# Issuing an expert's down product behind the next expert's gate-up product, in a fused decoder layer with 32 experts

## What is computed

```python
def expert_step(acc, params):
    wgu, bgu, wd, bd, g = params
    hgu = xt @ wgu + bgu
    gate = jnp.minimum(hgu[:, :D_EXPERT], SWIGLU_LIMIT)
    up = jnp.clip(hgu[:, D_EXPERT:], -SWIGLU_LIMIT, SWIGLU_LIMIT)
    y = ((up + 1.0) * (gate * jax.nn.sigmoid(SWIGLU_ALPHA * gate))) @ wd + bd
    return acc + g[:, None].astype(y.dtype) * y, None
```

## Time and profile before

| | |
|---|---|
| median of three runs | 1309.89 us (1307.11 to 1310.67) |
| span of the profiled execution, first to last instruction | 1304.8 us |
| median above that span | 5.1 us |
| PE busy | 1151.2 us (88%) |
| DVE busy, ACT busy | 207.3 us (16%), 210.2 us (16%) |
| read from memory over the span | 435.74 MB, 335 GB/s |
| mean granted TensorE clock | 0.937 of full speed |

### The profile page before, as it was taken

The page is one execution under the profiler, slowest core; times in us unless marked ns, Lnnn a source line. Parts: engine busy times, 40 slices in busy tenths (PEclk is TensorE's granted clock), DMA queues, the critical chain, the costliest instruction groups (busy, mean ns, idle before and its releaser), DMA issues.

```text
span 1304.8 us, 15767 instructions
## 1 busy us (share of the span) xinstructions
PE 1151.2 (88%) x6100; PEld 472.1 (36%) x6100; DVE 207.3 (16%) x424; ACT 210.2 (16%) x356; POOL 18.6 (1%) x68
## 2 busy tenths in 40 slices
PE   7999999878888888888888888888888888888884
PEld 6675444433333333333333333333333333333331
DVE  1301222231111111111111111111111111111112
ACT  2363230211111111111111111111111111111111
POOL 1010000000000000000000000000000000000000
PEclk9999999979899989999998999899989998999897
DMA  9913324339999999999999999999999999999970
GB/s 336 354 65 129 128 85 160 147 113 386 399 399 397 398 401 393 395 405 401 396 400 395 393 395 395 409 397 387 399 402 397 396 403 403 405 394 399 401 308 33
DMA packets 86624, 437.04 MB, mean 335 GB/s; under 512 B 7704, under 2 KB 7760, under 8 KB 53744
## 3 DMA queue, kind: packets, MB, share of 16 engines
q1 hardware_dynamic: 84880, 434.19, 83.8%
q10 hardware_dynamic: 1424, 1.57, 0.5%
q0 software_dynamic: 304, 1.06, 0.2%
HBM read 435.74 MB, written 1.06 MB: 335 GB/s over the span
## 4 chain that ended last, share of the span: by engine, by line
PE 88%; DVE 7%; ACT 4%; issue 1%; DMA 0%; DVEq 0%; SPq 0%; ACTq 0%
PE bank L984 35%; PE bank L1010 22%; PE bank L818 6%; PE bank L958 5%; PE bank L815 4%; PE bank L949 4%; PE bank L901 2%; PE bank L912 2%; DVE gates L758 2%; DVE gates L760 2%; DVE gates L754 2%; PE bank L1001 2%; ACT gates L545 2%; ACT gates L547 1%; PE bank L978 1%
## 5 line engine op out<-in xcount | busy, mean ns | idle before, releaser
L984 PE MATMUL bank<-ring,gates 128*64 128x512 f32 x2048 | 460.1, 596 | 0.0
L1010 PE MATMUL bank<-ring,gates 128*64 128x512 f32 x1024 | 286.9, 724 | 22.0 <-ACT gates L547 22.0
L984 PEld LDWEIGHTS bank<-ring,gates 128*64 128x64 f32 x2048 | 140.9, 137 | 252.1 <-issue 244.9
L754 DVE TENSOR_SCALAR gates<-bank 128x512 f32<-128x512 f32 x32 | 22.1, 691 | 862.0 <-PE bank L984 862.0
L1010 PEld LDWEIGHTS bank<-ring,gates 128*64 128x64 f32 x1024 | 84.0, 166 | 205.3 <-issue 174.7
L1001 PE MATMUL bank<-ident,gates 128*128 128x128 f32 x128 | 21.1, 289 | 95.9 <-DVE gates L760 95.9
L818 PE MATMUL bank<-ring,colsT 128*128 128x512 f32 x192 | 85.0, 596 | 0.0
L545 ACT ACTIVATE gates<-gates 128x512 f32<-128x512 f32 x32 | 20.1, 629 | 398.7 <-DVE gates L754 398.7
L958 PE MATMUL bank<-gates,scatter_w 64*128 64x512 f32 x264 | 65.6, 615 | 0.7 <-ACT gates L550 0.7
L550 ACT ACTIVATE gates<-bank 128x512 f32<-128x512 f32 x32 | 19.1, 597 | 290.2 <-PE bank L1010 290.2
L949 PEld LDWEIGHTS bank<-onehot,qkT 128*128 128x128 bf16 x1584 | 49.1, 99 | 28.7 <-issue 26.0
(11 more groups left out here) (168 smaller groups left out, 501.2 us busy)
## 6 DMA issues: line engine op xcount, KB each, us to landing
ring<-in_w_gate_up_dram SPq DMA_DIRECT2D x256, 1024.0 KB, 9.0
ring<-in_w_down_dram SPq DMA_DIRECT2D x128, 1024.0 KB, 7.1
ring<-in_w_in_dram SPq DMA_DIRECT2D x10, 2048.0 KB, 18.9
ring<-in_w_out_dram SPq DMA_DIRECT2D x1, 4096.0 KB, 13.7
ring<-in_w_proj_sb_dram SPq DMA_DIRECT2D x1, 2048.0 KB, 7.6
ring<-in_w_proj_moba_dram SPq DMA_DIRECT2D x1, 2048.0 KB, 13.4
resid<-in_x_dram SPq DMA_DIRECT2D x2, 512.0 KB, 3.7
bias<-u_scratch POOLq DMA_DIRECT2D x1, 1024.0 KB, 12.6
```

What stands on the lines that cost most here:

```text
L754: V.tensor_scalar(gate_t, bank[4][:, :], SWIGLU_LIMIT, None, ALU.min).then_inc(gate_rd, 1)
L984: ins = mm(bank[4 + i][SLOTS * c:SLOTS * (c + 1), :], xeT[:, k, :], ring[:, k, i * D + c * CH:i * D + (c + 1) * CH], start=False, stop=k = ...
L1010: ins = mm(bank[6][SLOTS * c:SLOTS * (c + 1), :], rows, ring[:, KD + s, j * D + c * CH:j * D + (c + 1) * CH], start=k == 0, stop=k == KD - 1)
```

## The change

The down product of expert e-1 is issued behind the gate-up product of expert e. PE first does the gate-up products of experts 0 and 1, then down 0, gate-up 2, down 1 and so on; after the loop come the transposes, scatter and down product of the last expert. Scatter now lags two experts behind. The transposes of weights and of h go to bank 7, which the gather uses too, and PE waits for the copy out of it (`gT_rd`, `hT_rd`) after two further steps of gate-up. `slot_used` is split into `gu_used` and `dn_used`, and SP loads gate-up of e+1 and then down of e. On DVE, the spreading of the token weights (`slot_weights`) is for expert e-1; on ACT the copies of weights and of hT are for e-1 too, ahead of the sigmoid of e. The table load of ACT's sigmoid stands once ahead of the loop, no longer in it. The number of matmuls and of loads is the same; two MEMSETs are gone.

```diff
+            def load_gate_up(e, done, first=0):
+                for k in range(first, KD):
+                    sp.wait_ge(gu_used, (e + done) * KD + (k + 1 - KD))
+                    load_slot(e, k)
+
+            def load_down(e, done):
+                for q in range(RING - KD):
+                    sp.wait_ge(dn_used, (e + done) * (RING - KD) + (q + 1 - RING + KD))
+                    load_slot(e, KD + q)
+
+            def experts(done):
+                load_gate_up(1, done)
+                with sp.Fori(1, E - 1) as e:
+                    load_gate_up(e + 1, done)
+                    load_down(e, done)
+                load_down(E - 1, done)
...
             def experts(done):
-                with act.Fori(0, E) as e:
...
+                nc.scalar.activation(stat[:, 63:64], stat[:, 6:7], ACT.Sigmoid)
+                gate_sigmoid(done)
+                with act.Fori(1, E) as e:
+
+                    token_weights(e + (done - 1))
+                    hidden_columns(e + (done - 1))
+                    gate_sigmoid(e + done)
+                    expert_rows(e + (done - 1))
...
+                with dve.Fori(1, E - 1) as e:
                     one_hots(e + 1).then_inc(onehot_rd, 1)
...
+                    slot_weights(e - 1, done)
+                    hidden(e, done, True)
+                    next_tokens(e + 1, done)
...
+            def expert(g, scatters, more):
+
+                gate_up(g, (0, 1))
+                if scatters:
+                    scatter_rows(g - 2)
+                weight_columns(g - 1)
+                gate_up(g, (2, 3))
+                pe.wait_ge(gT_rd, g)
+                hidden_columns(g - 1)
+                gate_up(g, (4, 5))
+                pe.wait_ge(hT_rd, g)
+                if more:
+                    gather(g + 2)
+                gate_up(g, (6, 7))
+                if scatters:
+                    pe.wait_ge(y_rd, g - 1)
+                down(g - 1)
...
+                gate_up(done, (0, 1, 2, 3, 4))
+                gather(done + 2)
+                gate_up(done, (5, 6, 7))
+                expert(done + 1, False, True)
+                with pe.Fori(2, E - 1) as e:
+                    expert(e + done, True, True)
+                expert(done + (E - 1), True, False)
+                pe.wait_ge(gT_rd, done + (E - 1))
+                hidden_columns(done + (E - 1))
+                scatter_rows(done + (E - 2))
+                pe.wait_ge(hT_rd, done + E)
+                weight_columns(done + (E - 1))
+                down(done + (E - 1))
+                scatter_rows(done + (E - 1)).then_inc(scattered, 1)
```

More of the change, by code:

```diff
@@ L245, in hybrid_layer @@
         xe_rd = sem("xe_rd")
-        slot_used = sem("slot_used")
+        gu_used = sem("gu_used")
+        dn_used = sem("dn_used")
         gate_rd = sem("gate_rd")
@@ L259, in hybrid_layer @@
         pass_step = sem("pass_step")
+        spread_rd = sem("spread_rd")
         pass_base = sem("pass_base")
@@ L325, in _, with another_pass @@
                 load_slot(0, s)
[L327 to L335, removed]
+            def load_gate_up(e, done, first=0):
[12 more added lines that the diff above has]
+                load_down(E - 1, done)
+            def another_pass(r):
+                load_gate_up(0, r * E)
+                load_down(0, r * E)
+                experts(r * E)
+            experts(0)
+            more_passes(sp, another_pass)
             sp.wait_ge(out_rd, 1)
@@ L535, in _, with token_weights @@
             nc.scalar.activation(pieces[2], res2, ACT.Copy).then_inc(piece_rd, 1)
-            def experts(done):
-                with act.Fori(0, E) as e:
[L540 to L550, removed]
+            def token_weights(g):
+                act.wait_ge(gT_ps, g + 1)
+                nc.scalar.activation(stat[:, 61:62], stat[:, 6:7], ACT.Sigmoid)
+                nc.scalar.activation(scatter_w[:, :, :], bank[7][:, 0:T].rearrange("p (t s) -> p t s", t=NT),
+                                     ACT.Copy).then_inc(gT_rd, 1)
@@ new lines, in hidden_columns, with gate_sigmoid, expert_rows @@
+            def hidden_columns(g):
+                act.wait_ge(hT_ps, g + 1)
+                nc.scalar.activation(hT[:, :, :], bank[7][:, :].rearrange("p (c s) -> p c s", c=4), ACT.Copy
+                                     ).then_inc(hT_rd, 1)
+            def gate_sigmoid(g):
+                act.wait_ge(gate_rd, g + 1)
+                nc.scalar.activation(sig_t, gate_t, ACT.Sigmoid, scale=SWIGLU_ALPHA).then_inc(sig_rd, 1)
+            def expert_rows(g):
+                act.wait_ge(dn_used, g * (RING - KD) + (RING - KD))
+                nc.scalar.activation(y_t, bank[6][:, :], ACT.Copy).then_inc(y_rd, 1)
@@ new lines, in experts @@
+                next_tokens(0, done)
+                one_hots(1).then_inc(onehot_rd, 1)
+                hidden(0, done, False)
+                next_tokens(1, done)
+                with dve.Fori(1, E - 1) as e:
+                    one_hots(e + 1).then_inc(onehot_rd, 1)
+                    slot_weights(e - 1, done)
+                    hidden(e, done, True)
+                    next_tokens(e + 1, done)
+                slot_weights(E - 2, done)
+                hidden(E - 1, done, True)
+                dve.wait_ge(gT_ps, done + (E - 1))
@@ L764, in experts @@
+                slot_weights(E - 1, done)
                 dve.wait_ge(scattered, passes + 1)
@@ L960, in scatter, with gate_up @@
                 return ins
+            def gate_up(g, ks):
+                if ks[0] == 0:
+                    pe.wait_ge(sel_rd, g + 1)
+                    pe.wait_ge(xe_rd, g + 1)
+                    for i in range(2):
+                        for c in range(2):
+                            mm(bank[4 + i][SLOTS * c:SLOTS * (c + 1), :], expert_sel[:, :],
+                               bgu[:, i * D + c * CH:i * D + (c + 1) * CH], start=True, stop=False)
+                for k in ks:
+                    pe.wait_ge(slot_in[k], g * 16 + 16)
+                    for i in range(2):
+                        for c in range(2):
+                            ins = mm(bank[4 + i][SLOTS * c:SLOTS * (c + 1), :], xeT[:, k, :],
+                                     ring[:, k, i * D + c * CH:i * D + (c + 1) * CH], start=False,
+                                     stop=k == KD - 1)
+                    ins.then_inc(gu_used, 1)
@@ new lines, in scatter_rows, with weight_columns, hidden_columns @@
+            def scatter_rows(g):
+                pe.wait_ge(y_rd, g + 1)
+                pe.wait_ge(gT_rd, g + 1)
+                return scatter()
+            def weight_columns(g):
+                pe.wait_ge(weighted_rd, g + 1)
+                for t in range(NT):
+                    ins = tp(bank[7][:, t * P:(t + 1) * P], onehot_g[:, t, :], ident[:, :])
+                ins.then_inc(gT_ps, 1)
+            def hidden_columns(g):
+                pe.wait_ge(h_rd, g + 1)
+                for c in range(4):
+                    ins = tp(bank[7][:, c * P:(c + 1) * P], h_t[:, c * P:(c + 1) * P], ident[:, :])
+                ins.then_inc(hT_ps, 1)
@@ new lines, in down @@
+            def down(g):
+                pe.wait_ge(hT_rd, g + 1)
+                for s in range(RING - KD):
+                    pe.wait_ge(slot_in[KD + s], g * 16 + 16)
+                    for j in range(2):
+                        k = 2 * s + j
+                        rows = hT[:, k % 4, SLOTS * (k // 4):SLOTS * (k // 4) + SLOTS]
+                        for c in range(2):
+                            ins = mm(bank[6][SLOTS * c:SLOTS * (c + 1), :], rows,
+                                     ring[:, KD + s, j * D + c * CH:j * D + (c + 1) * CH], start=k == 0,
+                                     stop=k == KD - 1)
+                    ins.then_inc(dn_used, 1)
@@ L962, in experts @@
             def experts(done, r):
-                base = 0 if r is None else r * (E + 1)
-                gather(base + 1)
+                gather(done + 1)
                 if r is None:
@@ L972, in experts @@
                                stop=True)
[L973 to L1013, removed]
```

64 lines of the change are left out of this document (30 added, 34 removed).

## The result

The changed kernel takes 1242.83 us in the median of four runs (1241.16 to 1244.82), the kernel before 1308.5 in the same comparison: ratio 0.950, 95% interval 0.948 to 0.952. The forecast was 1238 in a range of 1222 to 1272. The profiled execution took 1241.16 us with a span of 1239.3.

A forecast was written before the change was run, and what follows sets the result against it. PE bounded the kernel before, and the transfers at 420 GB/s would bound it after. First landing 286.3 + 926.3 of queue + 1.8 + 15.3 + 3 of allowances gave a span of 1233, plus 5.1 made 1238 us, range 1222 to 1272.

The forecast's parts named there:

- the prediction's check of 32.0: PE's time per expert before, summed as 18.4 + 4.4 stall + 7.0 down product + 2.2 clock, against 31.58 us in the chain.
- PE's own pace afterwards: PE's time per expert after the change without waits for weights: 18.4 + 1.0 + 7.0 = 26.4 us.
- first reissue: The first load issued again into a freed ring slot, at 281.5 us as before, landing 4.8 us later at 286.3.
- behind the down product: What follows the last expert's down product until the span ends, 15.3 us, taken over from the kernel before.
- lower clock at the end: Allowance of 2 us for the last slot and scatter running at PE's lower clock.
- the 926.3 us for 389.0 MB at 420 GB/s: Time for the remaining loads after the first has landed, at the rate read over 817:843 where a backlog stood.
- The bounds of 410 and 425 GB/s for this case: Rates assumed for transfers as the bound, giving 949 to 915 us of queue and 1222 to 1262 us; chance 74%.
- the 5.1 us carried over: Median time of 1309.89 less profiled span of 1304.8 before, added to the forecast span to give the time.
- The limit at 398 GB/s (1): Rival: transfers give no more than 398 GB/s over long stretches, so 977 us of queue and 1289 us; 8%.
- the new wait of PE (2): Rival: PE waits x us per expert for bank 7 or xeT, hidden below 3.6; 7% part gain, 3% no change.
- The clock (3): Rival: idle pieces between slots hold PE at 1.2 GHz, hidden up to 7 us per expert, 1360 at 14; 5%.
- That the wait for h might remain (4): Rival excluded beforehand: h(e-1) is made beside the down product of e-2 and needed after four slots of next gate-up.

The follow-up runs named there:

- removing the clock's part alone: Kernel before with 12 filling matmuls, result thrown away, on PE in front of its wait for h, nothing moved: 1247.70 us, ratio 0.953.
- the comparison run: The changed kernel once more, unaltered, on the same chip as the runs with 8 KiB down pieces and moved b_down matmuls: 1245.10 us, ratio 0.950.
- Half of the filling: Kernel before with 6 filling matmuls in place of 12 on PE in front of its wait for h: 1309.94 us, ratio 1.000.

## Why the prediction was right

**PE was the bound before, not the transfers:** right, shown by the halved bytes. The stall and the clock had about the sizes given: removing the clock's part alone gave 1.98 us per expert against 2.2 worked out. The 9.92 us of the expert read was the longest of a pattern of four that repeats in the chain before (8.4, 9.9, 8.8, 8.7; mean 9.0). The mean is 1.9 above 7.1, and with 1.9 for 2.2 most of the gap between the prediction's check of 32.0 and 31.58 closes.

**PE's own pace afterwards:** 25.87 us, forecast 26.4. In the chain the down product takes 6.87 instead of 7.0 and the transposes of h 0.59 instead of 1.0; the 0.2 for changing pattern in that 1.0 had no row behind it and none shows it. The ways through bank 7 and to xeT stayed hidden. Only the second expert, which has no down product in front of it, waited 3.6 us for xeT; the prediction did not see that.

**The transfers become the bound, and the sum goes along the queue:** right. The sum, term by term:

| Term | forecast | measured |
|---|---|---|
| first reissue | 281.5 | 281.6 |
| last landing (1213.9 + 8.2; forecast with 1 of allowance) | 1212.6 + 1 | 1222.1 |
| last slot | 1.8 | 1.9 |
| behind the down product | 15.3 | 15.3 |
| lower clock at the end | 2 | 0 |
| span | 1233 | 1239.3 |

The last issues of SP's queue and their landings, then the last down product:

```profile
L315 SPq DMA_DIRECT2D ring<-in_w_down_dram x4: 368/374/382, 1206.3 to 1213.9; - x4
...
DMA to landing us min/median/max: 8.1/8.2/8.2
```

```profile
1216.80 7.16 PE L1049 MATMUL bank<-ring,gates 128*64 128x512 f32 x32
```

The term that was mis-sized is the 926.3 us for 389.0 MB at 420 GB/s; it took 935.8. The rate over the long run was 418, which is 4.3 us. A part of this is the mix: the window of the earlier trace rows held some 8 gate-up and 2 to 3 down loads, more gate-up than the 2 to 1 of an expert, and down loads go at 410 against 421; that mix would give 419, and the last GB/s stays open. The thin stretch at 303 to 317 cost 2 x (1 - 61/418) + 12 x (1 - 377/418) = 2.9 where 1 was allowed. The rest, some 2 us, lies in the last loads, when the queue is no longer full: the last three us to 1222 carry 340, 160 and 29 GB/s (not tested by itself). The 2 us for a lower clock at the end were not needed. The misses partly cancel, 6.3 us of span in all. The bounds of 410 and 425 GB/s for this case had no rows behind them; down loads by themselves do go at 410, and 425 was not reached (418 over 400:1150, 422 over 1180:1200).

**That the gain is more than the pace:** right. 31 x (31.58 - 30.14) = 45 us of the 65.5 us of span come from the pace. The other 21 come from the end: from the last issue to the end of the span it was 46.1 us before (1258.7 to 1304.8) and is 25.4 now (1213.9 to 1239.3), since the last loads are used as they land.

**From the span to the time:** the 5.1 us carried over was not an overhead. The profiled run after took 1241.16 for a span of 1239.3, and a run of the kernel before with halved bytes 1310.77 for 1309.0: 1.9 and 1.8. The other 3.3 of the 5.1 are there because the profiled execution before was of the quick variant, with b_down at full clock, and its median was not. The changed kernel's profiled execution was of the same quick variant, and its median of four is 3.5 above its span. So 1.6 of the 6.3 us were hidden by luck, and the median was missed by 4.8. The first reissue at 281.5 came true for the same reason; in the comparison run it was at 285.5.

**Rivals.** The limit at 398 GB/s (1) and the new wait of PE (2) are out by the queue's 418 and PE's 25.87. The bound of 3.6 us below which (2) calls a wait hidden doesn't follow from its own sum: 295 + 31 x (26.4 + x) + 25 passes the forecast span of 1233 at x of about 3, since PE's path has its own start and end; the 7 us of (3) likewise become 6. The clock (3) did the opposite: granted full speed, 1.00, over 305:1215. That the wait for h might remain (4) was rightly excluded. A rival that the prediction does not have is SP: in the changed kernel its issues fill nearly the whole period (see the last section). It is out too. The loads land 17.7 to 26.6 us behind their issue, so some 7 or more loads stand in the queue; if SP's issuing were the bound, they would not pile up. A quarter fewer pieces (8 KiB for down) shortened the period by 1% only. The clock was forecast at 0.97 or more and is 1.00 over 400:1150.

What the prediction lacked is how little of the change is needed. It took 5.7 us per expert off PE (31.58 to 25.87), of which the queue lets 1.4 through, and the fall of the clock alone was 2.0.

## What to carry to other kernels

When an engine paces the transfers, the mean rate and the busy share of the DMA engines say nothing about their limit: read the rate where a backlog stands, multiply by all bytes, and set that beside the engine's pace without its stalls. If the two are close, a cheap filling of the stall can be worth as much as a reordering; but here it had to fill nearly the whole wait, and half of it was worth nothing. Once the queue bounded, three things made the time: when its first reissue leaves, its rate with the pieces it is given, and what stands behind its last landing. And the loads have to be reordered together with the work that frees their slots.

## What the runs showed of the hardware

Issuing a load can itself take long. SP needed 0.38 us for a down load before, and in the changed kernel, with 17.7 to 26.6 us from issue to landing, that is some 7 to 10 loads of 2.5 us in flight, the issues on SP took (min/median/max in ns, window 400:1180):

```profile
L310 SPq DMA_DIRECT2D ring<-in_w_gate_up_dram x208: 840/1030/5094, 410.5 to 1176.6; - x104
...
L315 SPq DMA_DIRECT2D ring<-in_w_down_dram x104: 849/4018/4181, 400.3 to 1178.0; - x104
...
DMA to landing us min/median/max: 17.7/22.6/26.6
```

So the chain of the changed kernel names SPq with 47% of the span, more than PE. In the turn from 862.75 us on, the eight gate-up issues last 13.68 us and the four down issues 15.14, of a period of 30.14. It cost nothing here, since the queue stayed full. The issues are long only where it is full: with the loads in the old order, where the queue ran dry in each turn, the same issues took 0.33 and 0.37 us. A kernel that issues small loads behind such a queue may have to wait for SP; no run here has one. With the down loads in pieces of 8 KiB, half as many, the median time to landing rose from 22.6 to 26.6 us: more loads were in the queue at a time. That the number of pieces in flight is what is limited fits both, and is not shown.

PE's clock fell behind idle time of 1.6 + 0.7 us around four short transposes, in every expert as before, and not behind 0.3 + 0.7 (granted clock 0.93 and 1.00 over 400:1200). Half of the filling had no effect at all on the time.
